# Three chunks of a depthwise convolution moved to products on ScalarE and sums on GpSimd

## The reference, cut to what matters

```python
def conformer_conv(h, pw1_w, pw1_b, dw_w, dw_b, ln_g, ln_b, pw2_w, pw2_b):
    u = h @ pw1_w + pw1_b                      # 1024 -> 2048
    a, gate = jnp.split(u, 2, axis=-1)
    u = a * jax.nn.sigmoid(gate)
    u = lax.conv_general_dilated(u, dw_w[:, None, :], window_strides=(1,),
        padding=((CONV_WIDTH - 1, 0),), feature_group_count=D_MODEL) + dw_b   # 31 causal taps per channel
    u = jax.nn.silu(layernorm(u, ln_g, ln_b))
    return u @ pw2_w + pw2_b                   # 1024 -> 1024
# then, in reference():
#   x = x + conformer_conv(rmsnorm(x, ...), ...)
#   x = x + swiglu(rmsnorm(x, ffn_norm_g[0]), ...)
```

## Time and profile before

| | us |
|---|---|
| median of 2 runs | 2307.36 (2307.05 to 2307.67) |
| the profiled execution | 2304.78 |
| its span | 2303.0 |
| TensorE busy, matmuls | 2245.9 (98%) |
| VectorE busy | 1673.9 (73%) |
| ScalarE busy | 903.6 (39%) |
| GpSimd busy | 68.7 (3%) |

### The profile page before, as it was taken

One profiled execution on the slowest core, in us unless ns is written; L12 is line 12 of the kernel. 1 busy time (PEld: TensorE's weight loads), 2 busy tenths in 40 slices (PEclk: granted clock), 3 DMA queues, 4 the chain that ended last, 5 costly groups with the idle time before them and its releaser, 6 DMA issues.

```text
span 2303.0 us, 27743 instructions
## 1 busy us (share of the span) xinstructions
PE 2245.9 (98%) x10517; PEld 1822.7 (79%) x10517; DVE 1673.9 (73%) x2617; ACT 903.6 (39%) x1603; POOL 68.7 (3%) x51
## 2 busy tenths in 40 slices
PE   7999989999999999999999999999999999999998
PEld 6885768888888888887777777878788888877887
DVE  6998589999666634345677777774778888977875
ACT  5221532222344423223455555564443233324443
POOL 0000000000000000002111111000000000000000
PEclk9999999999999999999999999999999999999999
DMA  4110223333333333332111111121023333338642
GB/s 142 47 37 19 74 74 92 101 90 99 92 95 97 95 101 89 103 90 84 37 38 38 37 38 38 62 60 44 28 78 95 98 113 99 113 101 305 202 155 110
DMA packets 287666, 202.13 MB, mean 88 GB/s; under 512 B 9045, under 2 KB 254126, under 8 KB 287534
## 3 DMA queue, kind: packets, MB, share of 16 engines
q1 hardware_dynamic: 287534, 200.36, 28.4%
HBM read 174.37 MB, written 25.95 MB: 87 GB/s over the span
## 4 chain that ended last, share of the span: by engine, by line
PE 89%; DVE 8%; ACT 1%; issue 1%; DMA 1%; SPq 0%; DVEq 0%; ACTq 0%
PE ps L2306 27%; PE ps L2308 27%; PE ps L2307 26%; PE ps L2444 3%; PE ps L2289 3%; DVE cacc L1655 2%; DVE cvA L1655 2%; PE ps L2402 1%; DVE sc L1906 1%; DVE Wl L1580 0%; ACT sc L1305 0%; PE ps L2361 0%; DVE Sl L1821 0%; PE ps L2371 0%; DVE rstd L1593 0%
## 5 line engine op out<-in xcount | busy, mean ns | idle before, releaser
L2306 PE MATMUL ps<-Sh,Wl 128*128 128x512 f32 x1616 | 655.5, 406 | 16.7 <-DVE Sl L1743 7.2
L2308 PE MATMUL ps<-Sh,Wh 128*128 128x512 f32 x1616 | 632.4, 391 | 0.0
L2307 PE MATMUL ps<-Sl,Wh 128*128 128x512 f32 x1616 | 631.7, 391 | 0.0
L2306 PEld LDWEIGHTS ps<-Sh,Wl 128*128 128x128 f32 x1616 | 305.0, 189 | 94.9 <-issue 33.2
L2308 PEld LDWEIGHTS ps<-Sh,Wh 128*128 128x128 f32 x1616 | 304.4, 188 | 65.8
L2307 PEld LDWEIGHTS ps<-Sl,Wh 128*128 128x128 f32 x1616 | 305.2, 189 | 59.5 <-issue 3.4
L1580 DVE TENSOR_TENSOR Wl<-raw,Wh 128x1024 fp32r<-128x1024 f32 (+1 forms) x178 | 213.4, 1199 | 87.3 <-ACT Wh L1092 86.0
L1092 ACT ACTIVATE Wh<-raw 128x1024 fp32r<-128x1024 f32 (+1 forms) x178 | 183.2, 1032 | 153.0 <-DMA raw<-in_ffn_w_dram 126.0
L2306 PE MATMUL ps<-G0h,Wl 128*128 128x512 f32 x352 | 138.6, 394 | 0.0
L2308 PE MATMUL ps<-G0h,Wh 128*128 128x512 f32 x352 | 137.0, 389 | 0.0
L2307 PE MATMUL ps<-G0l,Wh 128*128 128x512 f32 x352 | 137.0, 389 | 0.0
(11 more groups left out here) (279 smaller groups left out, 3862.9 us busy)
## 6 DMA issues: line engine op xcount, KB each, us to landing
raw<-in_ffn_w_dram SPq DMA_DIRECT2D x130, 512.0 KB, 3.8
raw<-in_pw_w_dram SPq DMA_DIRECT2D x32, 512.0 KB, 4.0
raw<-in_ffn_w_dram SPq DMA_DIRECT2D x32, 448.0 KB, 3.7
draw<-in_ffn_w_dram SPq DMA_DIRECT2D x55, 256.0 KB, 4.0
raw<-in_ffn_w_dram SPq DMA_DIRECT2D x36, 256.0 KB, 4.2
graw<-t_dram SPq DMA_DIRECT2D x36, 256.0 KB, 4.2
graw<-g_dram SPq DMA_DIRECT2D x33, 256.0 KB, 4.5
g_dram<-st SPq DMA_DIRECT2D x27, 256.0 KB, 2.0
```

The lines of the kernel that those rows point to most:

```text
L2306: pe.matmul(dst, ll, rh, start=start, stop=False)
L2307: pe.matmul(dst, lh, rl, start=False, stop=False)
L2308: return pe.matmul(dst, lh, rh, start=False, stop=stop)
```

## The change

Half A's convolution is now divided like this: VectorE does chunks 0, 1, 3, 5 and 7 as before (`CONV_V`); chunks 2, 4 and 6 (`CONV_G`) are made by two engines. ScalarE writes for each tap the product `up * w` (`taps`; the first two go to `cvA` and `cg`, the other 29 to a ring of 4 buffers `tap`), and GpSimd adds each of the 29 to `cvA` or `cg`, both in SBUF, and at the end the two together: 30 adds of 128x512 for a chunk. The diagonal matrices and TensorE's convolution are gone. `IN_BANKS` is empty, so VectorE's two accumulators are still `cvA` and `cacc` in SBUF.

The pair (5, B) is taken out of its place. Its two weight blocks are loaded a second time (`AGAIN`) behind those of the second product, and TensorE makes its two results behind the 8 of PW2A, with the sum of the RMS norm's squares (`sum_up`) inside the first of them. The ring's slots (`slot`, `slot_before`) and the counters of results follow. All pairs now take turns on the same four banks and two `tmp` buffers, whatever their half. The transposes of the small vectors (biases, gains, taps) come behind those of the first three blocks of x instead of ahead of all.

```diff
 PW1 = 0
 PW2A = PW1 + 2 * KC
-F0A = Ffn(0, (LA,), (8, 7, 7), PW2A + KC, 5 * KC, 0, 0, 0, True)
+AGAIN = PW2A + KC
+F0A = Ffn(0, (LA,), (8, 7, 7), AGAIN + 2, 5 * KC, 0, 0, 0, True)
...
 LATE = KC - 2
-CONV_PE = KC - 1
-DIAGS = 22
+BEHIND = LATE - 1
...
+PAIRS1 = [(n, hf) for n in range(BEHIND) for hf in (LA, LB)] + [(n, LA) for n in range(BEHIND, KC)] + \
+    [(n, LB) for n in range(LATE, KC)] + [(BEHIND, LB)]
+
+CONV_V, CONV_G = (0, 1, 3, 5, 7), (2, 4, 6)
+IN_BANKS = ()
+LOW_AT = {(0, 16): 4, (0, 24): 5, (1, 16): 6, (1, 24): 7, (3, 16): 10, (3, 21): 11, (5, 2): 14, (5, 7): 15}
+GLU_AT = {(0, 8): (0, LB), (0, 28): (1, LA), (1, 8): (1, LB), (1, 20): (2, LA), (3, 14): (3, LB), (3, 30): (4, LA),
+          (5, 13): (6, LA), (5, 28): (7, LA), (7, 13): (6, LB)}
+TAP_BUFS = 4
...
+            for m, n in enumerate(CONV_G):                    # GpSimd
+                o = cvA[:, n, :]
+                for i in range(2, CW):
+                    dst = cg[:, :] if i % 2 else o
+                    pool.wait_ge(p_ok, m * CW + i + 1)
+                    if i >= 4:
+                        pool.wait_ge(cg_s, m * (CW - 2) + i - 3)
+                    pool.tensor_tensor(dst, dst, tap[:, tap_slot(m, i), :], ALU.add).then_inc(cg_s, 1)
+                pool.wait_ge(cg_s, (m + 1) * (CW - 2))
+                pool.tensor_tensor(o, o, cg[:, :], ALU.add).then_inc(cg_ok, 1)
...
-            def diagonal(j):                                  # ScalarE
-                if j >= DIAGS:
-                    act.wait_ge(tap_mm, j - DIAGS + 1)
-                act.activation(diag[:, j % DIAGS, :], ident[:, :], ACT.Copy,
-                               scale=dw[:, j * KC + CONV_PE:j * KC + CONV_PE + 1]).then_inc(diag_ok, 1)
...
+            def taps(n, i0, i1):                              # ScalarE
+                m = CONV_G.index(n)
+                for i in range(i0, i1):
+                    j = i // 2 + (TAPS0 if i % 2 else 0)
+                    wj = dw[:, j * KC + n:j * KC + n + 1]
+                    src = upA[:, n, j:j + HT]
+                    if i == 0:
...
+                    elif i == 1:
+                        if m:
+                            act.wait_ge(cg_ok, m)
+                        act.activation(cg[:, :], src, ACT.Copy, scale=wj).then_inc(p_ok, 1)
+                    else:
+                        k = m * (CW - 2) + i - 2
+                        if k >= TAP_BUFS:
+                            act.wait_ge(cg_s, k - TAP_BUFS + 1)
+                        act.activation(tap[:, tap_slot(m, i), :], src, ACT.Copy, scale=wj).then_inc(p_ok, 1)
...
             for n in range(KC):                               # ScalarE, PW2A
-                hi(PW2A + n + 2)
+                if n < KC - 1:
+                    hi(PW2A + n + 2)
                 squares(SUM_F0A, n, X(n, LA), x_ok, n + 1)
+            hi(AGAIN + 1)
             act.activation(spare, eps, ACT.Sqrt)
+            hi(F0A.block0)
             root(1, LA, SUM_F0A)
...
-            for n in range(CONV_PE):                          # VectorE
+            for n in CONV_V:
+                if n == 3:
+                    glu(2, LB)
+                    lo(8)
+                    lo(9)
+                    glu(3, LA)
+                if n == 5:
+                    glu(4, LB)
+                    lo(12)
+                    lo(13)
+                    glu(5, LA)
                 for i in range(CONV_OPS):
...
+                    if (n, i) in LOW_AT:
+                        lo(LOW_AT[n, i])
+                    if (n, i) in GLU_AT:
+                        glu(*GLU_AT[n, i])
+                    conv(LA, n, i)
...
             add_square(SUM_F0A, KC - 1)
+            lo(AGAIN + 1)
+            lo(F0A.block0)
             recip(1, LA)
...
             for n in range(LATE, KC):                         # TensorE
                 pw1_pair(n, LA)
...
-            for j in range(CW):
-                pe.wait_ge(diag_ok, j + 1)
-                pe.matmul(ps[:, 6, :], diag[:, j % DIAGS, :], upA[:, CONV_PE, j:j + HT], start=j == 0,
-                          stop=j == CW - 1).then_inc(tap_mm, 1)
-            for n in range(LATE, KC):
+            for n in range(4):
                 mean(LA, n)
             pw1_pair(LATE, LB)
+            for n in range(4, KC):
+                mean(LA, n)
+            pw1_pair(KC - 1, LB)
             sum_up(SUM_LN_A)
-            pw1_pair(CONV_PE, LB)
...
-            sum_up(SUM_F0A)
+
+            def sum_beside(k):
+                if k == 4:
+                    sum_up(SUM_F0A)
+
+            for what in range(2):
+                dense(AGAIN + what, 6 + what, Sh[:, LB], Sl[:, LB], KC, cv_ok, len(CONV_V), None if what else sum_beside)
```

More of the change, by code:

```diff
@@ L947, in _ @@
                 load(PW2A + n, cols(pw2, n))
+            load(AGAIN, cols(pw1, KC + BEHIND))
+            load(AGAIN + 1, cols(pw1, BEHIND))
             ffn(F0A)
@@ L1137, in pad @@
                 act.activation(upB[:, n, 0:PAD], upA[:, n, HT:UP], ACT.Copy).then_inc(pad_ok, 1)
[L1139 to L1145, removed]
-                    if n in (1, 2):
-                        x_copies(8 * (n - 1) + 4 * hf)
-                pad(n)
-                if n == 3:
-                    for j in range(DIAGS):
-                        diagonal(j)
@@ new lines, in _ @@
+            hi(2)
+            gate(0, LA)
+            hi(3)
+            gate(0, LB)
+            pad(0)
+            hi(4)
+            act.wait_ge(lam_s, 2)
+            act.activation(lexp, lsum, ACT.Exp).then_inc(lam_e, 1)
+            gate(1, LA)
+            x_copies(0)
+            hi(5)
+            gate(1, LB)
+            x_copies(4)
+            pad(1)
+            hi(6)
+            gate(2, LA)
+            x_copies(8)
+            hi(7)
+            taps(2, 0, 10)
+            gate(2, LB)
@@ new lines, in _ @@
+            x_copies(12)
+            pad(2)
+            hi(8)
+            hi(9)
+            taps(2, 10, 19)
+            gate(3, LA)
+            taps(2, 19, CW)
+            gate(3, LB)
+            pad(3)
+            hi(10)
+            hi(11)
+            gate(4, LA)
+            pad(4)
+            taps(4, 0, 9)
+            gate(4, LB)
+            hi(12)
+            hi(13)
+            taps(4, 9, 18)
+            gate(5, LA)
+            hi(14)
+            hi(15)
+            pad(5)
@@ L1162, in mean @@
+            taps(4, 18, 27)
+            gate(6, LA)
+            pad(6)
+            taps(4, 27, CW)
+            taps(6, 0, 6)
+            gate(7, LA)
+            pad(7)
+            taps(6, 6, 15)
+            gate(6, LB)
+            taps(6, 15, CW)
             def mean(hf):
@@ L1708, in _ @@
             add_square(SUM_LN_A, KC - 1)
+            glu(KC - 1, LB)
             recip(0, LA)
@@ L1726, in _ @@
             for n in range(KC):
-                lo(PW2A + n + 2)
+                if n < KC - 2:
+                    lo(PW2A + n + 2)
                 pw2_out(LA, n)
@@ L2336, in pw1_results @@
                     else:
-                        free, value = (u_ok if what else sig_ok), pair(n - 1, hf) + 1
-                    dense(gate_block(n) + what, 2 * hf + what, Sh[:, hf], Sl[:, hf], KC, free, value, ready)
+                        free, value = (u_ok if what else sig_ok), pair(n, hf) - 1
+                    dense(gate_block(n) + what, 2 * (pair(n, hf) % 2) + what, Sh[:, hf], Sl[:, hf], KC, free, value, ready)
                     ready = None
```

173 lines of the change are left out of this document (88 added, 85 removed).

## The result

| | us | to before |
|---|---|---|
| before, median of 2 runs | 2307.36 (2307.05 to 2307.67) | |
| after, median of 2 runs | 2351.73 (2351.53 to 2351.92) | ratio 1.0195 [1.0179, 1.0212] |
| forecast | 2326 (2296 to 2352) | 1.008 |

What follows compares the result with a forecast made beforehand. TensorE held 89% of the chain, level with VectorE from 42 to 192 us. Terms 16.8 - 1.1 + 3.0 = +18.7 on 2304.8 gave 2323.5; with the runs' median 2.6 above, 2326 us, range 2296 to 2352.

Steps and rivals of the forecast that it cites:

- The price of an add: Half A's convolution: a GpSimd add of 128x512 lasts 1.00 us, bounds 0.95 and 1.90.
- the dearer-add rival: GpSimd's adds with two full tiles cost more, over 1.37 us each; 2360 us at 1.45; chance 12%.
- Tc: Moment when half A's last convolved chunk is ready: 220.1 us before, forecast at 236.9, 16.8 later.
- The turns: In half A's convolution, 74.5 adds each hold VectorE for 0.745 us, 55.5 us in all.
- VectorE's three main waits: Waits ahead of chunk 3 and around chunk 5's two halves: 3.9, 5.4 and 6.2 us, sum 15.5.
- each 0.1 us more costs 7.5: Half A's convolution: each 0.1 us more per add adds 7.5 us, in the 74.5 places counted.
- Strict turns, and the hold of duration less 0.255: VectorE and GpSimd alternate on SBUF operands; an add holds VectorE for its duration less 0.255 us.
- the five stretches: Adds meeting VectorE: before chunk 3's blocks end, in chunk 3, blocks before 5, chunk 5, around 7; 74.5 in all.
- The start: Transposes of x ahead of the convolution: everything following comes 3.3 us earlier, bounds 2 and 3.9.
- Behind Tc: From Tc on: -1.1 us to the end of PW2A and +3.0 for the deferred pair (5, B).
- the way to the end of PW2A: From Tc through PW2A: 1.1 us shorter, with the operand setting the end.
- Both run at once: Rival: GpSimd's adds cost VectorE nothing in half A's convolution; 2280 us; chance 12%.

Runs made afterwards that it cites:

- e1: The kernel after plus a tail timing GpSimd and VectorE instructions; GpSimd's adds with two full operands took 722, 1262 and 2339 ns for 256, 512 and 1024 columns.
- e5: The kernel after with GpSimd's adds on 384 of their 512 columns, leaving out a quarter of these sums: 2329.6 us, ratio 1.0096 to before.
- e3: The kernel after with GpSimd's adds on 32 of their 512 columns, leaving out 15 of 16 parts of these sums: 2291.5 us, ratio 0.9934 to before.
- e2: The kernel after with the accumulators of VectorE's chunks 3, 5 and 7 back in PSUM banks: 2315.0 us, ratio 1.0036 to before.
- e6: Against after: VectorE convolves six chunks, GpSimd two; accumulators of chunks 3, 4, 5, 7 in PSUM; pair (5, B) in place: 2298.4 us, ratio 0.9966 to before.
- e4: The kernel after with the pair (5, B) back at its old place ahead of the convolution's end: 2346.3 us, ratio 1.0173 to before.
- e7: Against e6: PW2A's first two weight blocks are split ahead of the LayerNorm chain: 2294.7 us, ratio 0.9954 to before.

## Why the prediction was wrong, step by step

- **The price of an add: this is the step that failed.** It was "for an add: half of 1.90 is 0.95, with some fixed part 1.00". The halving was sound (1.04 at 512 for that form, e1), but the earlier trace rows are instructions whose second operand repeats a value, and an add with two full tiles takes 1.26 to 1.28. I had written this difference down as the dearer-add rival and then left it out of the likeliest value. e5 against after shows what it cost: 237.2 against 259.9, **22.7 us** of Tc. The turns are 20.5 of it (0.27 x 74.5 would be 20), the waits 3.4, and after's earlier start takes 1.2 back. VectorE's three main waits came to 7.6 + 6.1 + 8.8 = 22.5 in after and to 18.1 in e5; two of the three are for gates, and these stand behind products that need a buffer freed by an add. I had held them fixed in "each 0.1 us more costs 7.5"; by e5 and after it is 8.4.
- **Strict turns, and the hold of duration less 0.255: right.** 1.69 to 1.70 apart is 0.66 + 1.28 - 0.25. The full 1.28 would give 1.94. The Trainium skill, "SBUF — State Buffer", section "SBUF: two separate sides", has the lock held for the whole instruction; the runs show about 0.25 us less.
- **Where and how often they meet, and the waits: nearly right, and helped by luck.** I had 10, 15.5, 2, 21 and 26 meetings in the five stretches; after has 8, 15, 1, 22 and 24, so 70 instead of 74.5, and e5 has 66. In e5 the turns are 6.7 below my sum, while the waits are 4.4, the start 1.5 and the own work 1.1 above it. These cancel to 0.3. e3 shows that a meeting has next to no price beside its length.
- **The start: right, with a run's own spread.** The first product of TensorE is at 16.20, 3.0 earlier than in the earlier trace rows; I took 3.3. VectorE's convolution starts 3.0 earlier in after, but only 1.7 to 1.9 earlier in e2 to e6, where the granted clock was lower at that place.
- **Behind Tc: too low.** I had -1.1 + 3.0 = +1.9; it is 100.0 - 93.3 = **+6.7**. Two terms failed. The deferred pair costs 5.2 and not 3.0 (e4): I had left out its sigmoid, with the table load, and its multiplication. And the way to the end of PW2A is not 1.1 shorter but 1.5 longer (94.8 of e4 against 93.3). This 1.5 I put down to the first block of PW2A, whose low part TensorE waits for: taking that wait away brings 4.8 in e7, so it is large enough, but it was not taken away in after alone, and the four kernels with the same lists behind Tc (after, e2, e3, e5) have 100.0 to 102.3 there, so a term of 1.5 is not clear of their spread. I had taken the operand for the last to arrive, because the earlier trace rows had it so in a kernel in which TensorE was late.
- **The sum.** 18.7, 23.0 more in Tc (259.9 - 236.9) and 4.8 more behind it make 46.5, against 46.8 between the two spans.
- **The range and the rivals.** "Both run at once" fell in e2 and e3: the turns are real. The dearer add was right in kind, but its 1.28 lies between my own forecast (0.95 to 1.25) and the rival (over 1.37), in a gap to which I had given no chance of its own. That the result lies within 2296 to 2352 at all is luck: it does so by 0.3 us, and lies outside the forecast's own range of 2320 to 2345. With 74.5 turns at 1.28 my formula gives 2347; the rest is the 4.8 behind Tc, while the longer waits (7.9) and the fewer meetings (7.4) about cancel.

The Trainium skill, "GPSIMD Engine Reference", section 3.1, has 4,497 ns for a float32 add of 2048 elements. The straight line of e1 gives 0.18 + 2048 x 0.0021 = 4.48 us, though no run here has that size. My estimate from the page, a quarter of it, was 1.12 and left out the fixed part; it was still nearer to 1.26 than the row that I chose.

## What to carry to other kernels

When work goes to a second engine, first ask which engine it will take turns with: here some 70 meetings with adds of 1.3 us on an engine that was idle cost more than the 26.6 us of matmuls that were taken away, and placing the neighbour's accumulators in PSUM took 36 of the 44 us back. A price scaled from another shape must come from the same form of operands. A step that costs nothing while another engine is late (a weight block split in the middle of an operand) has to be priced again when a change makes that engine early. And a sum that comes out to 0.3 us has to be checked term by term before it is called right.

## What was not expected of the hardware

- GpSimd's two-operand instruction costs 2.1 ns a column with two full float32 operands and 1.67 with one that repeats a value over 128 columns, at the same fixed 0.18 us.
- VectorE's product of 512 float32 columns with one SBUF operand and a per-partition factor, 0.475 us alone, also takes turns with GpSimd (1.39 and 1.42 in the mean beside each other), while a multiply-add from SBUF into a PSUM accumulator does not (0.749 and 1.26). The Trainium skill, "VectorE: DVE Perf Modes", section "Mode 2×_2P — use both read ports for one tensor", says that such a one-source instruction from SBUF to SBUF uses both read ports; the pace (0.475 against 0.74 to 0.75) and the turns agree.
- Once, one multiply-add of VectorE was held for 12.6 us by ten adds in a row. In seven other meetings the engines alternated from VectorE's first instruction on. Not explained.
- Kernels with the same lists up to that place had a granted clock of 1.00 (after) or 0.66 to 0.68 (e2, e3, e5) from 15 to 20 us, where the first products are made, and at the lower one VectorE's convolution starts 1.1 to 1.3 later. The runs don't say why.
